# Expert rows of u and v copied side by side into one table in HBM, and gathered as one 8 KB row per step

## The reference, cut to what matters

```python
# per token: 8 heads, in each the 16 best of 128 x 128 = 16384 experts
idx = take(cidx, top_k(s1[:, None] + s2[None, :], 16))     # (tokens, 8, 16)
g   = softmax(top)
ue  = u[idx]                       # u, v: (16384, 1024) fp32, 4 KB a row, 64 MB a table
ve  = v[idx]
act = gelu(einsum('bd,bhkd->bhk', x, ue))
y   = einsum('bhk,bhkd->bd', g * act, ve)
```

## Time and profile before

| | us |
|---|---|
| median of 3 runs | 3901.08 (3897.99 to 3906.31) |
| the profiled execution | 3908.25 |
| its span | 3906.4 |

### The profile page before, as it was taken

One profiled execution on the slowest core, in us unless ns is written; L12 is line 12 of the kernel. 1 busy time (PEld: TensorE's weight loads), 2 busy tenths in 40 slices (PEclk: granted clock), 3 DMA queues, 4 the chain that ended last, 5 costly groups with the idle time before them and its releaser, 6 DMA issues.

```text
span 3906.4 us, 34773 instructions
## 1 busy us (share of the span) xinstructions
PE 3268.0 (84%) x9650; PEld 1626.8 (42%) x9650; DVE 2740.8 (70%) x6256; ACT 1053.7 (27%) x2508; POOL 2382.5 (61%) x2340
## 2 busy tenths in 40 slices
PE   8899799899898958778778878877877887788787
PEld 7687455443434423333333333433433333333331
DVE  5599663367876967777776777777777777767794
ACT  5222574121532212221212222221221222212221
POOL 6221233155545667777777777777777677777775
PEclk9899899999999979999999999999999999999999
DMA  6325554598889999999999999999999999999997
GB/s 210 111 59 140 151 149 168 190 365 321 305 321 340 346 396 409 409 410 409 409 409 409 398 409 410 402 401 409 405 397 409 403 408 404 409 393 403 403 405 301
DMA packets 439390, 1329.13 MB, mean 340 GB/s; under 512 B 68170, under 2 KB 104166, under 8 KB 439199
## 3 DMA queue, kind: packets, MB, share of 16 engines
q0 software_dynamic: 313344, 1140.99, 74.4%
q1 hardware_dynamic: 121034, 172.93, 13.8%
q10 hardware_dynamic: 4821, 12.99, 0.9%
HBM read 1283.17 MB, written 43.55 MB: 340 GB/s over the span
## 4 chain that ended last, share of the span: by engine, by line
DMA 37%; PE 22%; POOL 16%; issue 6%; DVE 1%; SPq 1%; ACT 0%; ACTq 0%; DVEq 0%; POOLq 0%
DMA late_v_rows<-in_peer_v,late_expert_idx 25%; POOL late_v_rows L2320 8%; POOL late_u_rows L2310 8%; PE open_sums_ps L1762 7%; DMA late_u_rows<-in_peer_u,late_expert_idx 6%; PE open_sums_ps L2437 6%; PE open_h_T_ps L1776 4%; DMA late_u_rows<-in_peer_u,late_twin_idx 2%; DMA late_v_rows<-in_peer_v,late_twin_idx 1%; PE open_q_and_scores_ps L2364 1%; PE open_sums_ps L1702 1%; DMA fox_T<-scr_y 1%; DMA scr_m<-open_gated 1%; SPq L1563 1%; DVE late_u_rows L2667 1%
## 5 line engine op out<-in xcount | busy, mean ns | idle before, releaser
L2437 PE MATMUL open_sums_ps<-late_v_rows,late_diag 128*128 128x512 f32 (+1 forms) x3336 | 1675.1, 631 | 483.1 <-DMA late_v_rows<-in_peer_v,late_expert_idx 423.9
L2667 DVE CUSTOM_DVE_ANT_0 late_u_rows<-late_u_rows,open_rows_ps 128x1024 f32<-128x1024 f32 x944 | 1151.3, 1220 | 692.9 <-DMA late_u_rows<-in_peer_u,late_expert_idx 656.3
L2437 PEld LDWEIGHTS open_sums_ps<-late_v_rows,late_diag 128*128 128x128 f32 (+1 forms) x3336 | 593.7, 193 | 1445.6 <-issue 1380.0
L2320 POOL DMA_INDIRECT late_v_rows<-in_peer_v,late_expert_idx x880 | 850.4, 966 | 347.6 <-issue 205.3
L2310 POOL DMA_INDIRECT late_u_rows<-in_peer_u,late_expert_idx x880 | 845.7, 961 | 278.8 <-issue 254.8
L2489 ACT ACTIVATE late_gelu<-late_dots 128x4 f32<-128x4 f32 x236 | 48.5, 205 | 1906.0 <-DVE late_dots L2667 1906.0
L1675 POOL DMA_INDIRECT open_u_rows<-in_peer_u,late_expert_idx x112 | 160.9, 1437 | 277.3 <-DVE late_dots L2099 146.5
L2483 ACT ACTIVATE late_diag<-identity,late_weights 128x128 f32<-128x128 f32 x770 | 246.0, 386 | 2.0 <-PE open_sums_ps L2437 1.4
L483 POOL TENSOR_TENSOR front_w_lower<-front_w_raw,front_w_upper 128x512 fp32r<-128x512 f32 x62 | 94.9, 1549 | 194.7 <-ACT front_w_upper L689 193.5
L1139 POOL TENSOR_SCALAR attn_probs<-attn_probs,attn_row_scale 128x256 f32<-128x256 f32 (+2 forms) x68 | 93.0, 1374 | 194.3 <-DVE attn_row_scale L1250 194.2
L868 DVE SCALAR_TENSOR_TENSOR front_x_and_conv_y<-front_conv_input_T,front_conv_taps,front_x_and_conv_y 128x1118 f32<-128x1118 f32 x120 | 170.7, 1423 | 2.1
(11 more groups left out here) (389 smaller groups left out, 4612.7 us busy)
## 6 DMA issues: line engine op xcount, KB each, us to landing
open_weight_columns<-in_w_in SPq DMA_DIRECT2D x96, 256.0 KB, 7.1
late_u_rows<-in_peer_u,late_expert_idx POOLq DMA_INDIRECT x880, 15.8
late_v_rows<-in_peer_v,late_expert_idx POOLq DMA_INDIRECT x880, 15.8
front_w_raw<-in_w_in SPq DMA_DIRECT2D x48, 256.0 KB, 5.4
scr_m<-open_gated SPq DMA_DIRECT2D x42, 256.0 KB, 6.5
open_weight_columns<-in_peer_w_q SPq DMA_DIRECT2D x32, 256.0 KB, 6.5
w_mem_o<-scr_m SPq DMA_DIRECT2D x14, 512.0 KB, 9.3
open_x_T<-scr_xT SPq DMA_DIRECT2D x9, 512.0 KB, 7.0
```

What stands on the lines that cost most here:

```text
L2320: pool.indirect_dma_start(v[m % V_RING][:], None, io["peer_v"][0], bass.IndirectOffsetOnAxis(ap=rows_of(m), axis=0)).then_inc(s_v[m % V_RI ...
L2437: ins = pe.matmul(acc[0:rows, h, :], diag[k % DIAGS][:, 0:rows], v[n % V_RING][:, h * BANK:(h + 1) * BANK], start=(at == (0 if t else AHEA ...
L2667: dve.tensor_tensor_reduce(u[n % U_RING][:], u[n % U_RING][:], h2_rows, 1.0, 0.0, ALU.mult, ALU.add, dots[:, n % COLS:n % COLS + 1]).then_ ...
```

## The change

A scratch table `pairs` of 16384 rows of 8 KB is made in HBM. Row i holds row i of u and behind it row i of v. It is filled by 64 DMAs from HBM to HBM, each 512 rows of 4 KB (2 MB), the halves u and v in turn, all issued by ACT between its other instructions: 31 in the front, 18 in the attention, 4 while the opening computes its first gates, 11 in the opening's steps 2, 10, 18 and so on. POOL waits once for all 64 before its first gather from the table. The opening's own steps still gather from u and v.

In the experts each step then has one gather of 128 rows of 8 KB into one of 8 buffers of 8 KB a partition (the 16 buffers of 4 KB took the same room). A buffer is free when the sum of its step is done. Groups are of 2 steps in place of 4, and the diagonals of a group come right behind its own weights, so that sums run about four steps behind the dots. PE's hooks are moved to 6 steps behind their step, `keep_sum` comes 4 steps after a tile's end in place of 8, and `vector_sum` 3 steps behind its dot in place of 13. Only 2 of the buffers are free before the opening ends (before, 3 u buffers), and 6 gathers may go before the wait for the opening's last sums.

```diff
+PAIR_RING, PAIRS_IN_MEMORY, PAIRS_AHEAD_OF_SUMS = 8, 2, 6
+PAIR_ROWS = 512
+FRONT_COPIES_FROM, ATTENTION_COPY_EVERY, UNIT_COPY_EVERY = 20, 6, 8
+EXPERT_GROUP = 2
+HOOKS_BEHIND = 6
-V_LAG, V_LAG_LAST = 12, 5
-SHARE, SHARE_AT, SHARE_LAG = 8, 3, 13
+SHARE, SHARE_AT, SHARE_LAG = 8, 3, 3
@@ PairTable
+    def copy(self, eng, pieces=1):
+        for _ in range(min(pieces, PAIR_COPIES - self.copied)):
+            half, at = self.copied % 2, self.copied // 2 * PAIR_ROWS
+            src = self.sources[half][at:at + PAIR_ROWS, :].rearrange("(i e) d -> e i d", e=16)
+            dst = self.table[at:at + PAIR_ROWS, half * D:(half + 1) * D].rearrange("(i e) d -> e i d", e=16)
+            eng.dma_start(dst, src).then_inc(self.ready, 16)
+            self.copied += 1
@@ front, ACT
+                    if g.i >= FRONT_COPIES_FROM and g.i % 3:
+                        c.pairs.copy(act)
@@ attention, ACT
+                    if n % ATTENTION_COPY_EVERY == 0:
+                        c.pairs.copy(act)
@@ opening, ACT
+            if n % UNIT_COPY_EVERY == 2:
+                c.pairs.copy(act)
@@ experts, POOL
+        c.pairs.wait(pool)
+            if by_vector(last):
+                pool.wait_ge(s_vsum, S0 + vector_sums(last) + 1)
+            elif last >= AHEAD_ROWS:
+                pool.wait_ge(s_sum, S0 + tensor_sums(last) + 1)
+            pool.indirect_dma_start(pairs_in[b][:], None, scr["pairs"],
+                                    bass.IndirectOffsetOnAxis(ap=rows_of(n), axis=0)).then_inc(s_pair[b], 16)
@@ experts, PE
+            if n - HOOKS_BEHIND >= AHEAD_ROWS:
+                chain(n - HOOKS_BEHIND)
@@ experts, ACT
-            if t and n == tile_end(t - 1) + 2 * GROUP:
+            if t and n == tile_end(t - 1) + 4:
                 keep_sum(t - 1)
-            if G > AHEAD_GROUPS:
-                diagonals(G - 1)
...
+            diagonals(G)
@@ experts, DVE
-            if n % GROUP == 1 and n > AHEAD_ROWS + GROUP:
-                weights(n // GROUP - 1)
+            if n % EXPERT_GROUP == 0 and n > AHEAD_ROWS:
+                weights(n // EXPERT_GROUP - 1)
```

108 lines of the change are left out of this document (52 added, 56 removed).

## The result

| | us |
|---|---|
| before, median of 4 runs | 3899.84 (3897.99 to 3906.31) |
| changed kernel, median of 4 runs | 4097.75 (4090.42 to 4098.86) |
| ratio | 1.0497, 95% interval 1.0483 to 1.0511 |
| the profiled execution of the changed kernel | 4090.42, span 4088.6 |

The changed kernel takes 198 us more, where the forecast had 12 more and its range ended at 3985. The side was right, the size was not.

What follows compares the result with a forecast made beforehand. Experts bound by moving rows at 409 GB/s, the 1390 us before by PE with its loads and stores. Terms -72 + 29 - 5 + 60 = +12 us gave 3913; the range reached from 3848 to 3985.

Steps and rivals of the forecast that it cites:

- Part 1: Experts' gathers: one of 8 KB rows takes 2.488 us against 2.564 for two of 4 KB, -72 us over 944 steps.
- Part 2: Experts' ring of 8 buffers: stalls at the copy of a tile's sums and the turn of h2, +29 us, bounds 0 and 60.
- the hold of 17.0 us against a budget of 15.3: New tile's first sum: its row is held 17.0 us after landing, 1.7 too long before the DMA engines run dry.
- Part 3: Kernel's end: at most four sums left when the last row has landed, -5 us, gain between 3 and 12.
- Part 4: 64 copies of 2 MB in front, attention and opening: 46 to 73 us more, taken as +60.
- the price: One copy of 2 MB takes 5.13 us at 409 GB/s, or 5.76 at the opening's mixed-traffic rate of 364.
- the rule that only what exceeds a DMA share of 1 costs: Ahead of the experts, copies cost 17 to 29, 16 to 24 and 13 to 20 us in three stretches.
- idle time behind a busy stretch: After front and attention: copies in 575 to 750 are free, and the empty 75 us may take up earlier excess.
- The copies vanish in the gaps: Idle time behind front and attention absorbs their excess, the opening's 13 us remain and stalls halve: 3852 us, chance 0.33.
- Copies at half the rate: Traffic in both directions costs twice, 11.5 us a copy, about +215 us in place of +60: 4068 us, chance 0.07.
- A row moved as two: Experts' 8 KB rows are cut into two packets, so the longer row gains nothing: +84, 3985 us, chance 0.09.
- More is held than I count: Experts' buffers: queries, routing and the two stalls meet, stalls cost 60 us: +43, 3944 us, chance 0.13.

Runs made afterwards that it cites:

- mending both waits: Changed kernel without copies, reading 8 KB rows of u; ACT copies a tile's sums at its first step, PE turns h2 four steps later: 3849.81 us.
- the first and the fourth group: Follow-up runs on chips where the kernel before takes 3902.75 and 3908.30 us: copies alone, experts alone, then the changed kernel repeated without and with two edits.
- the second and third: Follow-up runs on chips where the kernel before takes 4131.64 and 4144.56 us: waits mended, copies placed otherwise, and prices measured by themselves.
- the changed kernel with both edits: Changed kernel with all copies, a tile's sums copied at its first step and h2 turned four steps later: 4023.60 us, and 4024.56 on another chip.

## Why the prediction was wrong

**What bounds the kernel.** Right: the experts by the rate of rows, the parts ahead of them by PE with its loads and stores.

**Part 1, rows of 8 KB.** Right. A row goes as one packet and the undisturbed rate is 420 GB/s, 2.497 us a step in place of 2.564: 944 x 0.067 = 63 us gained, where I had 72. The Trainium skill, "DMA: Bandwidth & Descriptors", section "SWDGE vs HWDGE vs iDMA", prefers packets of at most 4096 B; here packets of 8 KB were taken as they are and moved 420 GB/s in place of 409, 2.7% more, and the rival that rested on a row cut in two falls.

**Part 2, a buffer is held longer.** The mechanism and both places were right, the size was not: 7.3 and 7.4 us a tile where I had 1.7 and 2.4, so some 100 us in seven tiles in place of 29 (mending both waits won 68 of them back). The step that failed is the hold of 17.0 us against a budget of 15.3. The hold measured 20.1: the new tile's first sum took 4.05 us in place of 1.95, since PE's granted clock had fallen to 0.50, its lower level, while PE waited, and five more rows took 13.6 us in place of 12.4. And from POOL's release to the row at DVE it was 5.6 us, not 4.6, which makes the budget 14.3. Three errors of 1 to 2 us each, on a difference of 1.7. What I took for a small overrun of a bound was a difference of two sums, each known to 2 us. For the turn of h2 no such sum was measured, only its wait and its dip.

**Part 3, the end.** 11 us gained, in the bounds of 3 to 12: from the last dot to the end of the span it was 23.8 us and is 12.7.

The experts by these: -63 + 103 - 11 = +29, beside +15 measured without copies; where the other 14 lie is open.

**Part 4, the copies.** This is the miss: +189 by itself, and 172 ahead of the experts in the changed kernel, where I had 60. Two steps failed.

The first is the price. I took 5.13 to 5.76 us a copy, from rows whose transfers have HBM at one end only. By itself a copy takes 6.7, and 7.0 in the front. My own working with 7.0 gives, for 250 to 400, 18 x 7.0 + 75 - 150 = 51; for 425 to 575, 13 x 7.0 + 99 - 150 = 40; for the opening, 11 x 7.0 + 317 - 360 = 34: 125 in place of 46 to 73. The prediction named this as a case for which no row speaks and gave 11.5 as the upper end, with a chance of 0.07 for the case; the price lay between, and I gave that between no chance at all. (By its own terms, 46 to 73 for the copies, the range written as -3 to +30 is -2 to +25.)

The second is the rule that only what exceeds a DMA share of 1 costs. Even at 7.0 it leaves 47 of the 172 us over, 33 of them in the front (84 late, 51 by the rule), 5 in the attention and 8 in the opening; and with half of the bytes, where it gives nothing even at 7.0, the time was 58 more. The prediction names the waits for small stores and loads, and puts no term for them into the sum. They are what the runs show in its place. In the front, stores of 128 KB that ACT must wait for (its stage has two places) landed in 12.2 us in place of 2.5, at a mean share of 0.93; in 100 to 500 ACT waited 143 us for such stores in place of 38. In the attention it was loads, of keys above all, that PE waited for, 48 us in place of 12, and its granted clock was 0.82 there in place of 0.92. How much of the late landing is full engines in short slices, and how much is turns taken with the copies at a share under 1, stays open. That idle time behind a busy stretch would take up part of the work was wrong too: the run with the front's copies alone gave back 10 of 81 us by the first expert dot.

**The rivals.** "The copies vanish in the gaps" fell on its own point of decision (less than 20 us of stretch in front and attention; it was 129). "Copies at half the rate" was nearest in time, 4068 beside 4098, but by luck: its price is 1.7 times too high, and its rule leaves out the delay. "A row moved as two" fell. "More is held than I count" was right in what it named, and the measured term of 103 us was 1.7 times its 60; which waits meet was not as it said, since each dip costs by itself.

## What to carry to other kernels

Price a transfer by a row that moves data between the same two memories; where the trace has none, the range must hold everything up to the far bound, not only the case at it. Background transfers can cost before the mean DMA share reaches 1 (here 30 us at 0.78 to 0.80): look for small stores with a ring of two behind them and for loads that are waited for, and ask what each of those waits becomes. Where a ring's budget and its hold differ by less than the error of either, forecast a stall and not its absence (here 7.3 us of transfer for a POOL wait of 13.4), and count that the first sums behind the wait run at TensorE's lower clock. And a hook that waits for another engine is to be placed by where that engine will be when the rows run as close behind as they now do: moving two of them by four steps gave 67 us.

## What the chip showed that I had not expected

**HBM to HBM.** 2.10 MB take 6.5 to 6.7 us with nothing beside them, where gathers of as many bytes take 5.0 to 5.1 at the full rate.

**Two kinds of chip.** The kernel before took 3900 to 3908 us beside the result, the first and the fourth group, and 4132 and 4145 beside the second and third. The parts ahead of the experts are the same there (with copies to rows that lie together moved to the end, the first expert dot is at 1370.8, in the kernel before on the other kind at 1373.4). The experts with two gathers a step of 4 KB rows take 2750.8 us from the first dot to the last in place of 2509.2; with one gather a step of 8 KB rows they take 2464.8 and 2463.3 (the changed kernel with both edits). POOL's waits in 300 us of such experts, from the run with the front's copies:

```profile
POOL late_v_rows L2345 <- issue: 29.5, 84, 4.1
...
POOL late_v_rows L2345 <- remote: 22.1, 10, 5.0
```

and the stretch itself, at 364 GB/s, where the kernel before moves 406 from 2000 to 2300 on a chip of the first kind:

```profile
2000.00:2300.00 300.00, 225.66 (x542) 103.11 (x541) 191.72 (x478) 61.27 (x157) 199.02 (x206) 0.90 0.97 364
```

POOL stops ten times for something that the profile doesn't name ("remote"), up to 5 us each, and these waits are not there in the same window of the kernel before on a chip of the first kind, nor with rows of 8 KB on the second. What it is stays open. It matters for the verdict: on such a chip the mended version with all its copies is 2.7% faster than the kernel before, and 2.9% slower on the other. For the changed kernel as it is, which wasn't run there, 4098 beside 4132 to 4145 would be an estimate from these.
